# An encoder layer with a mixture of experts on one core: experts in pairs, rounded gathers, residual in PSUM, grouped score products

## The reference, cut to what matters

```python
s = jnp.einsum('bqhmd,bkhmd->bhmqk', qblk, k) + bias      # 4 heads, 2 maps of 64, relative bias
...
h = rmsnorm(x, g_moe)
g_idx, g_p  = top-1 of 4 groups;  e_idx, e_w = top-2 of the 4 experts in the group
for e in range(16):
    a = jax.nn.silu(hf @ w_gate[e]) * (hf @ w_up[e])      # 1024 -> 512
    y = y + comb_dense[:, e:e + 1] * (a @ w_down[e])      # 512 -> 1024
x = x + y
return rmsnorm(x, g_final)
```

## Time and profile before

| | us |
|---|---|
| median of 3 runs | 574.68 |
| the profiled execution | 574.78 |
| its span, first to last instruction | 573.0 |
| PE busy | 544.7 |
| DVE busy | 251.8 |
| ACT busy | 190.9 |
| DMA, mean over the span | 262 GB/s |

### The profile page before, as it was taken

How to read it: one execution, slowest core, us unless ns; L and a number is a source line. 1 busy time by engine, 2 the same in 40 slices (tenths; PEclk the granted TensorE clock), 3 DMA queues, 4 the chain that set the end, 5 groups by cost and what they waited for, 6 DMA issues and landing times.

```text
span 573.0 us, 8076 instructions
## 1 busy us (share of the span) xinstructions
PE 544.7 (95%) x3278; PEld 374.2 (65%) x3278; DVE 251.8 (44%) x467; ACT 190.9 (33%) x337; POOL 22.1 (4%) x34
## 2 busy tenths in 40 slices
PE   8899997999999999999888889999999999999991
PEld 8899995777888888988878544444444444444430
DVE  4573599675678689856546101111111111111114
ACT  6443653543626455445551111111111111011112
POOL 2000013000030000000100000000000000000000
PEclk9999998999999999999996799999999999999996
DMA  7787544632555446558999299999999999999502
GB/s 236 223 294 221 151 138 137 201 98 84 189 165 182 167 157 180 185 183 273 387 395 394 94 332 363 396 393 391 393 394 395 395 395 395 395 393 392 229 1 77
DMA packets 73790, 149.86 MB, mean 262 GB/s; under 512 B 8278, under 2 KB 11540, under 8 KB 73748
## 3 DMA queue, kind: packets, MB, share of 16 engines
q1 hardware_dynamic: 73732, 149.28, 74.0%
q10 hardware_dynamic: 16, 0.00, 0.0%
HBM read 148.21 MB, written 1.05 MB: 261 GB/s over the span
## 4 chain that ended last, share of the span: by engine, by line
issue 47%; PE 42%; DVE 7%; DMA 2%; ACT 2%; POOL 0%; POOLq 0%; DVEq 0%; ACTq 0%
PE bank L1301 11%; PE bank L1303 11%; PE bank L1302 11%; DMA raw<-in_w_in 2%; DVE wl L849 2%; PE bank L1415 1%; PE bank L1413 1%; PE bank L1308 1%; PE bank L1324 1%; PE bank L1438 1%; DVE al L835 1%; ACT wh L542 1%; DVE xc L867 1%; DVE xc L865 1%; DVE big L1130 0%
## 5 line engine op out<-in xcount | busy, mean ns | idle before, releaser
L849 DVE TENSOR_TENSOR wl<-raw,wh 128x1024 fp32r<-128x1024 f32 (+1 forms) x80 | 95.3, 1212 | 43.2 <-ACT wh L542 41.8
L542 ACT ACTIVATE wh<-raw 128x1024 fp32r<-128x1024 f32 (+1 forms) x80 | 82.3, 1042 | 77.7 <-PE bank L1303 57.7
L1301 PE MATMUL bank<-wh,ah 128*128 128x512 f32 (+2 forms) x248 | 94.9, 383 | 3.0 <-DVE wl L849 2.9
L1303 PE MATMUL bank<-wh,al 128*128 128x512 f32 (+2 forms) x248 | 93.5, 377 | 0.0
L1302 PE MATMUL bank<-wl,ah 128*128 128x512 f32 (+2 forms) x248 | 93.3, 376 | 0.0
L1236 DVE TENSOR_TENSOR kT<-bank,normg 64x512 f32<-64x512 f32 x16 | 11.1, 694 | 100.6 <-ACT normg L758 100.6
L1301 PEld LDWEIGHTS bank<-wh,ah 128*128 128x128 f32 x248 | 47.1, 190 | 12.4 <-DVE wl L849 3.6
L1301 PE MATMUL bank<-ah,wh 128*128 128x256 f32 x176 | 50.7, 288 | 3.3 <-DVE wl L849 2.3
L1303 PEld LDWEIGHTS bank<-wh,al 128*128 128x128 f32 x248 | 47.0, 189 | 8.8
L1302 PEld LDWEIGHTS bank<-wl,ah 128*128 128x128 f32 x248 | 47.2, 190 | 8.0
L1302 PE MATMUL bank<-al,wh 128*128 128x256 f32 x176 | 49.8, 283 | 0.0
(11 more groups left out here) (317 smaller groups left out, 835.4 us busy)
## 6 DMA issues: line engine op xcount, KB each, us to landing
raw<-in_w_in SPq DMA_DIRECT2D x48, 512.0 KB, 4.8
gates<-in_w_exp_gate SPq DMA_DIRECT2D x17, 512.0 KB, 10.5
gates<-in_w_exp_up SPq DMA_DIRECT2D x17, 512.0 KB, 11.2
raw<-in_w_branch SPq DMA_DIRECT2D x12, 512.0 KB, 3.5
big<-in_w_exp_up SPq DMA_DIRECT2D x10, 512.0 KB, 11.6
ah_raw<-in_w_exp_gate SPq DMA_DIRECT2D x10, 512.0 KB, 12.5
al_raw<-in_w_exp_up SPq DMA_DIRECT2D x10, 512.0 KB, 12.1
raw<-in_w_exp_down SPq DMA_DIRECT2D x10, 512.0 KB, 11.1
```

Of the source, the lines that this page charges most:

```text
L542: act.activation(dst, src, ACT.Copy, scale=scale).then_inc(done, 1)
L849: dve.tensor_tensor(wl[:, n % RING, 0:sz], raw[:, n % RING, 0:sz], wh[:, n % RING, 0:sz].bitcast(F32), ALU.subtract)\
L1301: pe.matmul(dst, st[0], mv[0], start=start, stop=False, skip_group_check=True)
L1303: return pe.matmul(dst, st[1], mv[0], start=False, stop=stop, skip_group_check=True)
```

## The change

- **Scores:** of each head first the four products of queries and keys, the two maps in turn, then the four bias products.
- **Rows:** ACT rounds x times its scale (`rows_hi`), DVE takes the rest (`rows_lo`). The gain moves into the copies of the gathered columns.
- **Gather:** four experts at a time, 8 products of 256 columns in fp32r for a quarter of the features. The first group is gathered whole before the first expert; group g+1 during the last two experts of group g.
- **Pairs:** activations of two experts lie on the two partition halves and are turned over together (4 transposes); the selection is turned over for two experts (2 transposes), and the combining weights of the pair come with it (4 products of one column). Down is two experts late, not one, and gives half the width of the result for both experts, so its weights are loaded as half rows (2 KB of each 4 KB), expert beside expert.
- **Residual:** `keep_residual` puts x into the four banks by identity products in float32; the scatters add to it. The add at the end goes; ACT squares and DVE scales straight from PSUM.
- **Loads:** 34 slots instead of 36, two of them x itself, once it is kept. Six loads are issued early, one after each chunk from the branch's last two on, when the branch's columns are turned over.

```diff
+RAWX = 34
+EARLY = 6
...
+    for n in range(EXPERTS + lag):
+        if n < EXPERTS:
+            out += [("gu", n, q) for q in range(4)]
+        if n >= lag:
+            out += [("down", n - lag, j) for j in range(2)]
+    return out
+
+
+UNITS = expert_units(2)
...
-        cols = over_("ah0", "expert_cols", [P, PER, KD, CAP])
...
+        sel = over_("toep", "sel", [P, 2, T, PER * CAP], F32R)
...
+        rows_hi, rows_lo = over_("hm", "rows_hi", [P, T, D], F32R), over_("big", "rows_lo", [P, T, D], F32R)
...
+        HOMES = [(u, "y_cols") for u in (flat(zs), flat(o_rows), flat(bgate), flat(xr)[:, 0:CH], flat(xst), big[:, 2048:2048 + CH])]
...
+        HOMES += [(x[:, t, :], "x_kept") for t in range(T)]
...
+            def load_chunk(slot, c, units):
+
+                what, n, j = units[c // 2]
+                dst = HOMES[slot][0].rearrange("p (k n) -> p k n", k=2)
+                if what == "down":
+                    e, half = 2 * (n // 2) + c % 2, n % 2
+                    src = a["w_exp_down"][0, e][256 * j:256 * j + 256, 512 * half:512 * half + 512]
+                else:
+                    src = a[("w_exp_gate", "w_exp_up")[c % 2]][0, n][256 * j:256 * j + 256, :]
+                sp.dma_start(dst, src.rearrange("(k p) n -> p k n", p=P)).then_inc(arrived_x[slot // 2], 16)
...
+                if 0 <= n - FIRST["b21"] < EARLY:
+                    if n == FIRST["b21"]:
+                        sp.wait_ge(s_("cols_pe"), COLS["ssd"] + 2)
+                    load_chunk(n - FIRST["b21"], n - FIRST["b21"], UNITS)
...
+            for t in range(T):
+                hi_of(rows_hi[:, t, :], x[:, t, :], s_("rows_hi"), scale=rs[:, t:t + 1])
...
+                for i in range(2):
+                    kt = 2 * j + i
+                    ins = act.activation(cols[:, g % 2, kt, :], src[:, 256 * i:256 * i + 256], ACT.Copy,
+                                         scale=vecT[:, 42 + kt:43 + kt])
+                ins.then_inc(s_("cols_even"), 1)
...
+                act.activation(aT[:, :, :], bank[2][:, :].rearrange("p (k n) -> p k n", k=4), ACT.Copy).then_inc(s_("act_cols"), 1)
+
+            def sel_cols(p, count_):
+
+                act.wait_ge(s_("sel_T"), count_)
+                act.activation(combs[:, p % 2:p % 2 + 1], bank[2][:, 256:257], ACT.Copy).then_inc(s_("combs_ready"), 1)
+                act.activation(selT[:, :, :], bank[2][:, 0:256].rearrange("p (t n) -> p t n", t=T), ACT.Copy)\
                     .then_inc(s_("sel_cols"), 1)
...
+            for j in range(4):
+                act.activation(squares[j], bank[4 + j][:, :], ACT.Square, accum_out=ss4[:, 2 * (j % 2) + j // 2:2 * (j % 2) + j // 2 + 1])\
+                    .then_inc(s_("x_squares"), 1)
...
+                dve.wait_ge(s_("rows_hi"), t + 1)
+                dve.scalar_tensor_tensor(out=rows_lo[:, t, :], in0=x[:, t, :], scalar=rs[:, t:t + 1],
+                                         in1=rows_hi[:, t, :].bitcast(F32), op0=ALU.mult, op1=ALU.subtract).then_inc(s_("moe_rows"), 1)
...
+                for i in range(2):
+                    kt = 2 * j + i
+                    ins = dve.tensor_scalar(cols[:, g % 2, kt, :], src[:, 256 * i:256 * i + 256], vecT[:, 42 + kt:43 + kt], None, ALU.mult)
+                ins.then_inc(s_("cols_odd"), 1)
...
-            for half in range(2):
-                for t in range(T):
-                    xv = x[:, t, 512 * half:512 * half + 512]
-                    dve.tensor_tensor(xv, bank[4 + 2 * t + half][:, :], xv, ALU.add).then_inc(s_("x_out"), 1)
...
-                    dve.scalar_tensor_tensor(out=hm[:, t, c], in0=x[:, t, c], scalar=rs[:, t:t + 1], in1=gain_a[:, c],
+                    dve.scalar_tensor_tensor(out=hm[:, t, c], in0=bank[4 + 2 * t + half][:, :], scalar=rs[:, t:t + 1], in1=gain_a[:, c],
...
-                for m, dst in enumerate((pS1, pS0)):
-                    for t, w, lo in ((1, 256, 0), (0, 128, 128)):
-                        d = dst[:, 256 * (1 - t):256 * (1 - t) + w]
-                        pe.matmul(d, qT[QK * m:QK * m + QK, h, P * t:P * t + P], kT[QK * m:QK * m + QK, h, 0:w],
-                                  start=True, stop=False, skip_group_check=True)
-                        mm = pe.matmul(d, flip[:, :], toep[:, h, lo:lo + w], start=False, stop=True, skip_group_check=True)
+                blocks = [(t, w, lo, m, dst[:, 256 * (1 - t):256 * (1 - t) + w])
+                          for t, w, lo in ((1, 256, 0), (0, 128, 128)) for m, dst in enumerate((pS1, pS0))]
+                for t, w, _, m, d in blocks:
+                    pe.matmul(d, qT[QK * m:QK * m + QK, h, P * t:P * t + P], kT[QK * m:QK * m + QK, h, 0:w],
+                              start=(t == 1), stop=False, skip_group_check=True)
+                for t, w, lo, _, d in blocks:
+                    mm = pe.matmul(d, flip[:, :], toep[:, h, lo:lo + w], start=False, stop=True, skip_group_check=True)
                 mm.then_inc(s_("scores_pe"), 1)
...
+            def keep_residual(t):
+
+                for half in range(2):
+                    mm = pe.matmul(rest[2 * t + half][:, :], ident[:, :], x[:, t, 512 * half:512 * half + 512], start=True, stop=False,
+                                   skip_group_check=True)
...
-            keep_warm(WARM[7], rest[0])
+            keep_residual(0)
+            keep_warm(WARM[7], bank[0])
...
-            keep_warm(WARM[8], rest[0])
...
-            def gather(g, pair, r, dst):
-
-                for kk in range(4):
-                    for t in range(T):
-                        at = 4 * r + kk
-                        mm = pe.matmul(dst[:, P * kk:P * kk + P], hm[:, t, P * at:P * at + P], sel[:, g % 2, t, P * pair:P * pair + P],
-                                       start=(t == 0), stop=(t == T - 1))
+            keep_residual(1)
+            keep_warm(WARM[8], bank[0])
...
+            def gather(g, j, dst):
+
+                for i in range(2):
+                    kt = 2 * j + i
+                    for t in range(T):
+                        for rows in (rows_hi, rows_lo):
+                            mm = pe.matmul(dst[:, 256 * i:256 * i + 256], rows[:, t, P * kt:P * kt + P], sel[:, g % 2, t, :],
+                                           start=(t == 0 and rows is rows_hi), stop=(t == T - 1 and rows is rows_lo))
                 mm.then_inc(s_("gather_pe"), 1)
...
+            def sel_T(p):
+
+                g, at = p // 2, P * (p % 2)
+                for t in range(T):
+                    pe.transpose(bank[2][:, P * t:P * t + P], sel_f32[:, g % 2, t, at:at + P], ident[:, :])
+                for t in range(T):
+                    for i in range(2):
+                        n = 2 * p + i
+                        mm = pe.matmul(bank[2][row_half[i], 256:257], sel_f32[:, g % 2, t, at + CAP * i:at + CAP * i + CAP],
+                                       weight[:, t, n:n + 1], start=(t == 0), stop=(t == T - 1), skip_group_check=True)
+                mm.then_inc(s_("sel_T"), 1)
...
+                e, up, gate = n % PER, row_half[n % 2], row_half[1 - n % 2]
...
-                    pe.matmul(bank[0][0:CAP, :], cols[:, e, kt, :], gw[:, kk, :], start=(kt == 0), stop=(kt == KD - 1),
-                              skip_group_check=True)
-                    mm = pe.matmul(bank[0][CAP:P, :], cols[:, e, kt, :], uw[:, kk, :], start=(kt == 0), stop=(kt == KD - 1),
-                                   skip_group_check=True)
+                    st = cols[:, n // PER % 2, kt, CAP * e:CAP * e + CAP]
+                    pe.matmul(bank[0][gate, :], st, gw[:, kk, :], start=(kt == 0), stop=(kt == KD - 1), skip_group_check=True)
+                    mm = pe.matmul(bank[0][up, :], st, uw[:, kk, :], start=(kt == 0), stop=(kt == KD - 1), skip_group_check=True)
...
-                    mm = pe.transpose(bank[2][:, CAP * j:CAP * j + CAP], act_rows[:, P * j:P * j + P], ident[CAP:P, CAP:P])
+                    mm = pe.transpose(bank[2][:, P * j:P * j + P], act_rows[:, P * j:P * j + P], ident[:, :])
...
-                    for half in range(2):
...
-                        mm = pe.matmul(bank[1][CAP * half:CAP * half + CAP, :], aT[:, q, :],
-                                       HOMES[2 * slot + j][0][:, 512 * half:512 * half + 512], start=(q == 0), stop=(q == 3),
...
+                for kk in range(2):
+                    kt = 2 * j + kk
+                    for i in range(2):
+                        mm = pe.matmul(dst[row_half[i], :], aT[:, kt, row_half[i]], w[i][:, kk, :], start=(kt == 0), stop=(kt == 3),
...
-                            r = slice(CAP * half, CAP * half + CAP)
-                            mm = pe.matmul(bank[4 + 2 * t + half][:, :], selT[r, buf, t, :], part[r, :],
-                                           start=(first and part is yh), stop=True, skip_group_check=True)
+                        mm = pe.matmul(bank[4 + 2 * t + half][:, :], selT[:, t, :], part[:, :], start=False, stop=True,
+                                       skip_group_check=True)
...
```

(64 more changed lines are left out.)

305 lines of the change are left out of this document (101 added, 204 removed).

## The result

The changed kernel takes **553.6 us** (median of 4 runs, 553.1 to 555.72) against 574.93 us, a ratio of 0.9648 with a 95% interval of 0.9612 to 0.9683. The forecast was 554.0 (545 to 564). The profiled execution has a span of 551.9 us and a time of 553.85.

A forecast was written before the change was run, and what follows sets the result against it. The prediction took PE to bound the kernel before and the transfers after: S at 319.2 us plus 218.2 to the last landing (537.4), plus 5.6 and 9.3, is 552.3; with 1.8 us around it 554 us, range 545 to 564.

The forecast's parts named there:

- S: Moment of the first gate product, where the expert stage starts; forecast 320.97 - 6.4 + 4.6 = 319.2 us.
- Scores: Self attention's score products on PE: a head from 4.01 to 2.4 us, 6.4 us saved over four heads.
- Early loads: Six expert loads behind branch chunks on SP's queue: cost nothing, at most 2 us.
- Way to the first expert: Router to first gate product: residual products 1.4 and 2.3 us, gathers and DVE's copy 0.9, together 4.6 us later.
- Transfers: Expert stage: 158 loads, 82.8 MB at 390 GB/s, 212.4 us, plus 3 us; last landing at S + 218.2 = 537.4 us.
- PE's waits: End of the expert stage: PE waits for transfers from some 13 units before the end.
- A sign that was none: Expert stage: SP waiting for spent units past the first three experts was listed as showing the forecast wrong.
- The end: Behind the last landing: 5.6 us to the first add or square, then 9.3 us to the end of the span.
- PE stays the bound: Rival on the expert stage: PE still sets the end, with half rows at 410 GB/s; 547 us, chance 0.2.
- The front gives little: Rival on the part before the first expert: scores save nothing or clock stays low, S 325, 560 us; chance 0.2.
- The clock falls in the waits: Rival on the last 13 units: PE's clock drops while waiting for transfers, 579 us; chance 0.04.
- Half rows are slow: Rival on the down loads: half a 4 KB row costs as much as the whole, 205 GB/s, 627 us; chance 0.03.

The follow-up runs named there:

- a_no_early: Changed kernel with none of the first six expert loads issued early, all issued in the expert list instead; 554.06 us.
- a_residual_late: Changed kernel with the first half of the residual's float32 products moved from ahead of the first warming products to behind the rank products; 559.08 us.
- b_wide: Kernel before with two float32 identity products of 512 columns put between the router's products and the warming products behind them; 571.66 us, ratio 0.9938.
- a_whole_rows: Changed kernel with each down load fetching 128 whole 4 KB rows instead of 256 half rows (weights wrong, time alone read); 550.11 us.
- a_gather_some: Changed kernel with four of the twelve gathers in the expert loop, those of the second group, as float32 products; 557.97 us.
- a_scores_apart: Changed kernel with the self attention's score products back in their old order, each followed by its table product; 562.03 us.
- a_best: Changed kernel with earlier overflow test, no second warming stretch, scatter 14 inside the last down, and whole-row down loads for seven of eight pairs; 546.62 us.

## Why the prediction was right

The mechanism held: the bound passes from PE to the transfers, and what PE saves in the loop beyond that is worth nothing. But S was 3.5 us too late and the transfers 3.1 us too short in the forecast. That these two cancelled is luck, and so are the 0.4 us between forecast and result.

- **Scores**: 2.4 us a head forecast, 2.19 measured; 6.4 us in all against 7.3, and at the router's first product, counted from H, 6.9.
- **Early loads**: nothing, shown by a_no_early.
- **Way to the first expert: mis-sized.** From the router's first product to the first gate product I had 4.6 us more than before; it is 20.71 against 20.10 us, 0.6 more. The ranks come 9.08 us behind the router's first product for 8.44, and the first wide products have no part in it (1.4 forecast): it is 9.08 in a_residual_late too, which has none there. The wait for DVE hides them even at half clock. What stands behind the ranks grew by 1.80 (second wide products), 0.25 (gathers) and 0.78 (wait for the overflow test), and shrank by 0.82 and 2.05 us (ranks and warming products at full clock): nothing together, for 3.2 forecast. The failing step is "come when the clock is at the lower level": I carried the 0.50 of the earlier trace rows over to a stretch that now has wide products in it, and so left ranks and warming products at their old price. a_residual_late and b_wide show that link from both sides. S came at 315.74, not 319.2. It would have been 1 us earlier but for head 0, which began at 108.02 for 106.93; this is the H of the table, which lies between 106.54 and 111.05 in all profiles.
- **Transfers: mis-sized.** Forecast S + 218.2, measured 537.04 - 315.74 = 221.3 us. The first load waited 1.97 us for its slot (2.84 forecast). 82.8 MB at 387 GB/s are 214.0 us (212.4 at 390). The loss is 5.3 us for 3: about 2.0 in the ramp from 318 to 326 us (161, 366, 272 and 362 GB/s), and some 2.5 at the end, where the bytes left at 530 us (174 GB/s over 10 us) would need 4.5 us at full rate but were waited for until 537.04.
- **The rate by row length** stood in the text as 410 against 388 of two short stretches, and I took 390 for all. It is a term: 394 against 387, 5 us in E - S.
- **PE's waits**: in the last 13 units forecast; measured, 12 waits spread over the last 18 units.
- **A sign that was none**: I had named SP's waits for spent units past the first three experts as a sign of being wrong, and took the 85 us of the earlier trace rows as what decides that PE was the bound. The changed kernel's SP waits 34.1 us for them between 400 and 500 us, with the transfers at 387 GB/s all the while. A load takes about 11 us there from issue to landing, and its 0.524 MB are 1.35 us at that rate, so some eight loads are under way when SP waits for the next slot. What tells the bound is the other half of that reading: whether bytes or products end last, and whether PE waits for loads.
- **The clock behind S**: "first units at half clock" stood in the 3 us for the transfers; in this profile they ran at full clock.
- **The end**: from landing to the end of the span 14.9 us, as forecast (5.6 + 9.3); from the first square it is 551.9 - 542.95 = 8.95.
- **The Trainium skill** (DMA: Bandwidth & Descriptors, Where 436 GB/s comes from) would have had 358 GB/s and, by the prediction's estimate from that figure, 19 us more. The trace doesn't agree: one core held 387 GB/s over 200 us here, 394 in a_whole_rows. The same page's section Measured has 425 GB/s for a core that loads alone, as this one does; 387 and 394 lie between the two figures.

The rivals. *PE stays the bound* is refuted by the waits after 490 us, but a_gather_some shows how near it is. *The front gives little* fell with S at 315.74; its second half, that S comes through whole, is what a_scores_apart shows. *The clock falls in the waits* did not happen: PEclk is 1.00 from 490 to 530 us, with PE idle for a fifth of it. *Half rows are slow* is true in kind, at 2% of the whole rate (and by the estimate above 5% of a down load's) and not at half of it.

## What to carry to other kernels

When the bound passes from an engine to the transfers, write the end as start of the stream, bytes by rate, and a fixed end, and look for gains in these three alone, until the engine ends last again, as in a_best; before adding up an engine's savings, subtract what its new waits will take. A ring of slots couples the two: time that the stream loses early is never got back, so slack seen at the end can't be spent at the beginning. And don't price new products at the clock that the old ones left behind: wide ones may change it.

## What was not expected of the hardware

- Loads with rows of 4 KB in one load of three give 394 GB/s, with rows of 2 KB throughout 387, the same bytes and as many loads.
- Two float32 products of 512 columns behind products of 20 columns made the kernel before 3.6 us faster (b_wide; 1.1 us of it are to be seen in its profile), though they are 3.76 us of work. In ten profiles of ten with them the granted clock was 1.00 right behind the ranks, in three of three without them 0.50.
- Ahead of the ranks the clock's fall isn't the same in every execution of the same instructions: 1.00 from 298 to 306 us in the changed kernel, 0.68 in a_gather_some.

```profile
298.00:306.00 8.00, 8.00 (x31) 5.37 (x32) 6.70 (x29) 0.38 (x3) 0.00 (x0) 0.68 0.57 203
```
